# Softmax weights by tanh, and the accumulator read in the first slot of a tile

## What is computed

```python
def block(xb):                       # 128 tokens
    q = (xb @ w_q).reshape(p, 8, 2, 64)
    sc = jnp.einsum('phcd,hcnd->phcn', q, sub_keys)        # two scores of 128 keys, 8 heads
    top_s, top_i = lax.top_k(sc, 16)
    cand_s = top_s[:, :, 0, :, None] + top_s[:, :, 1, None, :]     # 256 pairs
    best_s, best_pos = lax.top_k(cand_s.reshape(p, 8, 256), 16)
    idx = take_along_axis(cand_i, best_pos)
    g = jax.nn.softmax(best_s, axis=-1)
    act = jax.nn.gelu(jnp.einsum('phkd,pd->phk', expert_u[idx], xb), approximate=False)
    return jnp.einsum('phk,phkd->pd', g * act, expert_v[idx])
```

## Time and profile before

| | |
|---|---|
| median of 3 runs | 1867.18 us (1865.82 to 1867.99) |
| profiled execution | 1864.53 us |
| its span | 1862.7 us |
| PE busy | 1598.0 us (86%) |
| DVE busy | 1501.8 us (81%) |
| POOL busy | 749.1 us (40%) |
| ACT busy | 427.5 us (23%) |
| mean DMA rate over the span | 335 GB/s |

### The profile page before, as it was taken

The page is one execution under the profiler, slowest core; times in us unless marked ns, Lnnn a source line. Parts: engine busy times, 40 slices in busy tenths (PEclk is TensorE's granted clock), DMA queues, the critical chain, the costliest instruction groups (busy, mean ns, idle before and its releaser), DMA issues.

```text
span 1862.7 us, 19074 instructions
## 1 busy us (share of the span) xinstructions
PE 1598.0 (86%) x4856; PEld 822.8 (44%) x4856; DVE 1501.8 (81%) x3370; ACT 427.5 (23%) x1040; POOL 749.1 (40%) x559
## 2 busy tenths in 40 slices
PE   8989999799978888887879888787888878888886
PEld 6878778677533333333333333333333333333332
DVE  5777886588768888888778888877888887888887
ACT  5223333354321211111211111121111112211111
POOL 1000000000014555655545666554556655555662
PEclk9999999899999999999989999999999999999999
DMA  8555472142239999999999999999999999999996
GB/s 305 181 215 180 160 277 95 51 169 80 91 119 393 421 421 422 422 422 421 409 400 409 422 422 422 421 402 397 413 422 422 422 422 389 422 422 422 422 422 254
DMA packets 93689, 623.97 MB, mean 335 GB/s; under 512 B 11441, under 2 KB 11441, under 8 KB 24241
## 3 DMA queue, kind: packets, MB, share of 16 engines
q0 software_dynamic: 78912, 570.46, 74.6%
q1 hardware_dynamic: 14704, 52.74, 7.8%
HBM read 621.06 MB, written 2.10 MB: 335 GB/s over the span
## 4 chain that ended last, share of the span: by engine, by line
DMA 34%; PE 30%; DVE 15%; DVEq 9%; issue 7%; ACT 4%; POOL 1%; POOLq 0%; ACTq 0%; SPq 0%
DMA arena<-in_experts,idx 32%; PE ps L624 8%; PE ps L412 6%; PE ps L413 6%; PE ps L414 6%; DVE arena L1303 5%; DVEq L1188 4%; PE ps L544 3%; DVE arena L1323 2%; POOL arena L401 1%; DVEq L1204 1%; DMA arena<-in_w_ada 1%; ACT L832 1%; PE ps L575 1%; ACT L836 1%
## 5 line engine op out<-in xcount | busy, mean ns | idle before, releaser
L624 PE MATMUL ps<-arena 128*128 128x512 f32 x2048 | 1017.0, 624 | 220.8 <-DVE arena L1323 198.7
L401 POOL DMA_INDIRECT arena<-in_experts,idx x512 | 727.9, 1422 | 767.7 <-PE ps L624 445.0
L624 PEld LDWEIGHTS ps<-arena 128*128 128x128 f32 x2048 | 356.1, 192 | 833.0 <-DVE arena L1323 548.5
L1303 DVE CUSTOM_DVE_ANT_0 arena<-arena,ada 128x1024 f32<-128x1024 f32 x512 | 627.4, 1225 | 88.6 <-DMA arena<-in_experts,idx 73.9
L832 ACT ACTIVATE arena<-arena 128x1 f32<-128x1 f32 x512 | 103.8, 203 | 1022.4 <-DVE arena L1303 1022.0
L1323 DVE TENSOR_SCALAR arena<-ident,arena 128x128 f32<-128x128 f32 x512 | 182.7, 357 | 48.0 <-ACT arena L832 43.0
L364 POOL DMA_DIRECT2D arena<-in_w_ada x24 | 12.9, 539 | 242.2 <-DVE arena L922 232.2
L412 PE MATMUL ps<-xT_hl,w_hl 128*128 128x512 f32 x192 | 78.1, 407 | 9.0 <-DVE xT_hl L886 9.0
L881 DVE TENSOR_TENSOR w_hl<-arena,w_hl 128x1024 fp32r<-128x1024 f32 x47 | 57.4, 1221 | 32.3 <-ACT w_hl L652 32.2
L413 PE MATMUL ps<-xT_hl,w_hl 128*128 128x512 f32 x192 | 76.2, 397 | 0.0
L414 PE MATMUL ps<-xT_hl,w_hl 128*128 128x512 f32 x192 | 75.9, 395 | 0.0
(11 more groups left out here) (223 smaller groups left out, 1693.3 us busy)
## 6 DMA issues: line engine op xcount, KB each, us to landing
arena<-in_w_ada POOLq DMA_DIRECT2D x24, 1024.0 KB, 5.2
arena<-in_w_in SPq DMA_DIRECT2D x44, 512.0 KB, 3.3
arena<-in_experts,idx POOLq DMA_INDIRECT x512, 14.6
arena<-in_w_out SPq DMA_DIRECT2D x14, 512.0 KB, 4.7
lnw<-in_w_in SPq DMA_DIRECT2D x8, 512.0 KB, 4.5
arena<-in_w_grp POOLq DMA_DIRECT2D x4, 1024.0 KB, 7.0
arena<-in_w_out SPq DMA_DIRECT2D x1, 4096.0 KB, 12.7
arena<-in_w_q SPq DMA_DIRECT2D x1, 4096.0 KB, 13.6
```

The source lines that it names most:

```text
L401: nc.gpsimd.indirect_dma_start(ring[:, n % RING, :], None, experts, bass.IndirectOffsetOnAxis(ap=idx[:, e, n:n + 1], axis=0)).then_inc(arr ...
L624: last = mm(ps[half][:, :], lhsT=diag[:, n % RING, :], rhs=ring[:, n % RING, DM + half * T:DM + (half + 1) * T], start=(e == 0 and n == 0) ...
L1303: nc.vector.tensor_tensor_reduce(out=urow, in0=urow, in1=h2cur, scale=1.0, scalar=0.0, op0=ALU.mult, op1=ALU.add, accum_out=dots[:, e, n:n ...
```

## The change

The softmax weight exp(x), with x = score minus the largest score, is written with the hyperbolic tangent: exp(x) = (1 + tanh(x/2)) / (1 - tanh(x/2)). ACT computes the tangent, DVE the quotient, the sum over 16 and the division by it (`gate_piece`, now in two pieces, in slots 7 and 8). The small pieces of DVE move: `pair_piece` 1 to 4 stand in slots 0 to 3, `index_piece` in 4 to 7, `key_piece` in 9 to 14, `pair_piece(0)` in 15. The query copy on ACT moves behind slot 4, the scores on PE behind slot 5, their copy on ACT behind slot 7. The output pieces 0 and 1 stand in slot 0 of the new tile instead of slot 1, and all output pieces stand ahead of the slot's diagonal instead of behind it. The mean square of the output is made in two halves after slots 1 and 2, the root after slot 5. At the end of the kernel pieces 0, 2, 1, 3 follow each other, and ACT squares the first half when it is ready.

```diff
             act.wait_ge(best_ready, 1)
-            nc.scalar.activation(best[:, :], best[:, :], ACT.Exp, accum_out=esum[:, :]).then_inc(exp_ready, 1)
+            nc.scalar.activation(best[:, :], best[:, :], ACT.Tanh, scale=0.5).then_inc(half_tanh, 1)
...
-                        if n == 4:
+                        if n == 5:
                             pe.wait_ge(q_copied, HEADS * t + h + 1)
                             pe.wait_ge(score_ready, 2 * HEADS * t + 2 * (h - 1))
...
+            def square_half(half, nth):
+                act.wait_ge(row_ready, nth)
+                c = slice(half * T, (half + 1) * T)
+                nc.scalar.activation(junk2[:, c], outb[:, c], ACT.Square, accum_out=stats[:, 13 + half:14 + half])
+                act.drain()
+                if half == 0:
+                    nc.scalar.activation(stats[:, 12:13], stats[:, 13:14], ACT.Identity, scale=1.0 / DM,
+                                         bias=stats[:, 15:16])
+            def root_of_halves():
+                act.drain()
+                nc.scalar.activation(stats[:, 14:15], stats[:, 14:15], ACT.Sqrt, scale=1.0 / DM,
+                                     bias=stats[:, 12:13]).then_inc(root_ready, 1)
...
+                    if row is not None and n in (1, 2):
+                        square_half(n - 1, row)
                     if n == 3:
+                        act.wait_ge(best_ready, step + 2)
+                        nc.scalar.activation(best[:, :], best[:, :], ACT.Tanh, scale=0.5).then_inc(half_tanh, 1)
+                    if n == 4:
                         copy_q(parity, 2 + parity, step + 3)
-                        act.wait_ge(best_ready, step + 2)
-                        nc.scalar.activation(best[:, :], best[:, :], ACT.Exp, accum_out=esum[:, :]).then_inc(exp_ready, 1)
-                    if n == 6:
+                    if row is not None and n == 5:
+                        root_of_halves()
+                    if n == 7:
                         act.wait_ge(score_mm, step + 3)
...
+            def gate_piece(piece, to):
+                plus, minus = tanhs[:, 0, :], tanhs[:, 1, :]
+                if piece == 0:
+                    ts(plus, best[:, :], 1.0, None, ALU.add)
+                    ts(minus, best[:, :], -1.0, 1.0, ALU.mult, ALU.add)
+                    dve.drain()
+                    nc.vector.reciprocal(minus, minus)
+                if piece == 1:
+                    dve.drain()
+                    nc.vector.tensor_tensor_reduce(out=plus, in0=plus, in1=minus, scale=1.0, scalar=0.0, op0=ALU.mult,
+                                                   op1=ALU.add, accum_out=esum[:, :])
+                    dve.drain()
+                    nc.vector.reciprocal(esum[:, :], esum[:, :])
+                    dve.drain()
+                    ts(gate[:, to, :], plus, esum[:, 0:1], None, ALU.mult)
...
             pair_piece(0)
-            pair_piece(1)
...
-            beside = {(0, 1): (0, 1), (0, 7): (2,), (0, 15): (3,), (1, 7): (4,), (1, 15): (5,)}
+            beside = {(0, 0): (0, 1), (0, 8): (2,), (0, 15): (3,), (1, 8): (4,), (1, 15): (5,)}
...
-                        if n < 3:
-                            pair_piece(n + 2)
-                        elif n < 7:
-                            index_piece(n - 3, 1 - e)
+                        if n < 4:
+                            pair_piece(n + 1)
+                        elif n < 8:
+                            index_piece(n - 4, 1 - e)
...
+                        if done is not None:
+                            for piece in beside.get((e, n), ()):
+                                output(done, piece)
                         dve.wait_ge(gelu_done, step * TOPK + n + 1)
                         ts(diag[:, n % RING, :], ident[:, :], acts[:, e, n:n + 1], gate[:, e, n:n + 1],
                            ALU.mult, ALU.mult).then_inc(diag_ready, 1)
-                        if done is not None:
-                            for piece in beside.get((e, n), ()):
-                                output(done, piece)
...
-            for piece in range(6):
+            for piece in (0, 2, 1, 3, 4, 5):
                 output(NT - 1, piece)
```

More of the change, by code:

```diff
@@ L205, in mixers_and_peer @@
         esum = sb("esum", [P, 1])
+        tanhs = sb("tanhs", [P, 2, TOPK])
         idx = sb("idx", [P, 2, TOPK], u32)
@@ L641, in _ @@
                             last.then_inc(score_mm, 1)
-                        if n == 5 and h == HEADS - 1:
+                        if n == 6 and h == HEADS - 1:
                             pe.wait_ge(h2n_ready, t + 1)
@@ L840, in act_step @@
                             nc.scalar.copy(cur[:, c, :], score_out(parity, c)).then_inc(score_ready, 1)
-                    if n == 2 and row is not None:
-                        root_of_squares(outb, junk2, row)
-                    if n == 9 and switch is not None:
+                    if n == 10 and switch is not None:
                         copy_h2T(switch + 2, 2)
@@ L857, in _ @@
                 act_step((NT - 1) * HEADS + e, e % 2, NT - 1 if e == HEADS - 3 else None)
-            root_of_squares(outb, junk2, 3 * NT)
+            square_half(0, 3 * NT)
+            square_half(1, 3 * NT + 1)
+            root_of_halves()
         @block.vector
@@ L1253, in _ @@
                 index_piece(piece, 0)
-            dve.wait_ge(exp_ready, 1)
-            gate_piece(0)
+            dve.wait_ge(half_tanh, 1)
+            gate_piece(0, 0)
+            gate_piece(1, 0)
+            dve.drain()
             make_h2(2)
```

32 lines of the change are left out of this document (14 added, 18 removed).

## The result

| | before | after |
|---|---|---|
| median | 1867.59 us (4 runs, 1865.82 to 1869.34) | 1898.43 us (4 runs, 1896.88 to 1899.81) |
| ratio after to before | | 1.0165, interval 1.0147 to 1.0183 |
| profiled execution, its span | 1864.53, 1862.7 us | 1898.01, 1896.2 us |
| DVE busy | 1501.8 us | 1520.6 us |
| ACT busy | 427.5 us | 344.4 us |

The changed kernel is 1.65% slower, 30.8 us by the medians. The forecast was 1858.1 us, range 1853.0 to 1864.0. What came is rival C, to which I gave 0.07.

The account below looks back on a forecast made before the run. It took the expert gathers' DMA rate, 422 GB/s, as the bound, with time lost only where gathers run short. Gains of 1.4 + 5.8 + 1.5 + 0.4 = 9.1 us off 1867.18 gave 1858.1 us, range 1853.0 to 1864.0.

Parts of the forecast that it names:

- rival C: DVE stalls at all eight inner-loop branches because the body grows: 31 us more, less 9.1, time 1889 us; chance 0.07.
- The inner branches, at nothing: DVE's branches back over two steps: no issue stall before, only 0.40 us for DMA, and no term in the sum.
- rival B: Only engines off the path get faster, so later releases gain nothing: no change, 1865.7 us; chance 0.12.
- Accumulator read: At a new tile's start, DVE reads the old accumulators in the first slot, PE starts 2.25 us earlier: 5.8 us won.
- Step 10: Behind the tile loop's branch back: branch pause stays, half the shortfall after slot 4 goes, 1.5 us for both places.
- Start: First slots of the expert stage: an index search leaves the way to the first dot, loads go; 1.4 us won.
- Table loads and new DVE work: Steady steps: removed ACT loads win nothing, and 1.0 us of new DVE work a step hides in free time.
- Tail: End of the kernel: half of the last square runs beside DVE, 0.63 us left instead of 1.06; 0.4 us won.
- step 8: Where the old tile's accumulators are read: gathers run short at three places, 7.44 us together.
- rival E: PE keeps its upper clock level after the shorter idle time at the accumulator read: 16 us won, 1851 us; chance 0.06.
- rival D: Tanh is not in gelu's table, so tables are still loaded: only 4.6 us won, time 1862.6 us; chance 0.02.

Follow-up runs that it names:

- a_pad32: The changed kernel with 32 empty DVE instructions (drains) ahead of the expert stage: 1867.08 us, ratio 0.9999 to the kernel before.
- b_read0: The kernel before with only the accumulator read and the output pieces moved as in the change: 1866.00 us, ratio 0.9993.
- b_tiles_read0: The kernel before with DVE's tile loop written out and the accumulator read in slot 0: 1859.94 us, ratio 0.9970.
- a_tiles: The changed kernel with 32 drains ahead of the expert stage and DVE's tile loop written out, inner loops kept: 1861.39 us, ratio 0.9964 to the kernel before.
- b_tiles: The kernel before with only DVE's tile loop written out, inner loops kept: 1859.04 us, ratio 0.9954.
- a_pad215: The changed kernel with 215 drains on DVE ahead of the expert stage: 1871.26 us, ratio 1.0028 to the kernel before.
- a_pad179: The changed kernel with 179 drains on DVE ahead of the expert stage: 1876.28 us, ratio 1.0060 to the kernel before.

## Why the prediction was wrong, point by point

**The inner branches, at nothing** are the step that failed: the sum has no term for them, and they cost 31 us. C's mechanism was named, with its place and price, and given 0.07 because "the free branch is half as long as the costly one, and the body grows by 5%". Both are true and neither decides. I compared lengths, where position decides, and counted 196 and 206 rows of the order, in which the drains (52 and 56), the match loads (18) and four semaphore instructions are missing: the body had 270 instructions and was, by the rule above, already long enough to be caught at some offsets. With a position not known, 27 starts in 256 for the first three tiles and as many for the last are some 0.2, against half that before. Its price was nearly right: 3.87 us an inner branch was forecast, 5.2 measured for six, 4.5 for two. Its sum of 1889 us was 9.4 short, since it took eight branches (31 us; six cost as much) less 9.1 us of gain that did not come. Without the pauses a_pad32 measures what rival B said, no change (1867.08 us, where B had 1865.7), and not the 1858.1 us of the forecast: the gain itself failed too, and the next points say where.

**Accumulator read, 5.8 us.** The mechanism was right and seen: PE idle for 2.43 us against the 2.8 expected, in the changed kernel and in a_pad32, windows at 422, 420 and 412 GB/s in a_pad32. As a gain in time it was over-sized: b_read0 gives 1.3 us (interval -0.7 to 3.4), and counted over the middle of the stage it is 1.2 with the tile branch and 1.9 and 2.7 without. What failed here is the adding up of shortfalls place by place, as if a place cured stayed won. In b_tiles_read0 a part of it is missing at the ends of the tiles, 80 us later; in a_tiles it is missing in a steady step. Why a place cured makes another short is open.

**Step 10, 1.5 us.** The 1.5 us did not come, and it went the other way: the windows at 960 and 1280 us are 372 and 371 GB/s in a_pad32, 381 and 383 before. My bounds, 0 and 3.0, left them no way to become worse.

**Start, 1.4 us.** Windows 48 to 88 us behind the stage's start are 3.3 us short in a_pad32 and 3.4 in the changed kernel, 3.5 before: 0.1 to 0.2. The timeline of the start in a_pad32 shows why releasing PE earlier bought so little (dots and gathers: start, us, idle before):

```profile
581.04 1.22 DVE L1339 CUSTOM_DVE_ANT_0 arena<-arena,ada 128x1024 f32<-128x1024 f32 x1
581.25 1.82 POOL L402 DMA_INDIRECT arena<-in_experts,idx  x1 [0.30 <-issue]
...
583.30 1.22 DVE L1339 CUSTOM_DVE_ANT_0 arena<-arena,ada 128x1024 f32<-128x1024 f32 x1
583.38 1.96 POOL L402 DMA_INDIRECT arena<-in_experts,idx  x1 [0.30 <-issue]
```

In the kernel before the gathers at 586.41 and 588.50 us lasted 1.19 and 1.30 us, behind 0.90 us of waiting for PE. With slots free, neither POOL (1.9 + 0.3 us a gather) nor DVE waits for another engine: the dots, too, start 2.1 to 2.3 us apart. Before, with POOL waiting 0.90 us each time, the gathers came 2.1 to 2.2 us apart as well. So DVE is enough to explain the pace, and whether POOL would hold it up too is not shown. A gather that starts within 0.25 us of a dot's start lasts 1.87 us in the median, in the kernel before and in the changed one; one that starts outside of any dot 0.94; those that start later in a dot lie between. The Trainium skill (GPSIMD Engine Reference, the row on SBUF interfaces) says that GpSimd shares its SBUF interfaces with VectorE, and contends for them with a VectorE instruction that has two SBUF inputs, as the dot has; the rows agree, and no run tried it. I had priced DVE and PE as pacers of a place that catches up, and left POOL out, which by these rows is as slow. That this is why the gain is lost in the middle of the stage too is argued, not shown.

**Table loads and new DVE work, nothing in a steady step.** Right. 8 loads are left in the stage, as forecast; the wait for the fifth gelu is gone; a window at 720 us of a_pad32 is at 422 GB/s with DVE at 34.51 of 40 us ("near 35"). The product with sum takes 177 ns, not 250. New work, loads gone and later query copy together cost 0.6 to 1.4 us over the stage by the table above, which is not told from nothing. The loads that went (most of 83 us of ACT) bought no time that the runs can tell.

**Tail, 0.4 us.** From PE's last end to the end of the span 9.5 us before, 9.3 after: 0.2. The second half of the square took 0.63 us, as forecast (timeline of the end, changed kernel):

```profile
1888.94 0.63 ACT L833 ACTIVATE arena<-arena 128x512 f32<-128x512 f32 x1 [0.30 <-DVE arena L1318]
```

**PE keeps its clock at step 8 (rival E).** Partly so. In a_pad32 the first four matmuls took 1.98 us after 2.43 us of idle time at two of the three step 8s (from 884.19 and 1209.57 us), and those windows are at 422 and 420 GB/s. At the third the clock fell to its lower level, and the window is at 412:

```profile
1534.68 5.40 PE L625 MATMUL ps<-arena 128*128 128x512 f32 x8 [2.44 <-DVE arena L1363]
```

The time that E promised for it did not follow, as for the read.

## What to carry to other kernels

When a change alters how many instructions an engine runs, count them as the engine executes them, drains and the extra loads that the trace shows included, for each loop body; by the rule above a body of more than 257 can stall at its branch at some offsets (270 to 336 long here, two of the four lengths did), and the same kernel with a few empty instructions ahead settles in one run whether it does. Here that was worth 31 us, more than anything the change meant to do, and writing out only the loop whose body is over 512 long was worth 8 us in the unchanged kernel. Where one shared rate (the gathers' DMA) bounds a stage, shortfalls cured place by place did not add up to time: sum the windows of the whole stage before and after, and ask who paces the recovery.

## What the runs showed of the hardware that I had not expected

- A held branch cost DVE 4.8 to 6.1 us while the gathers filled the DMA engines. Each cost the kernel 4.5 to 5.2 us at an inner branch and 4.1 at the tile branch (b_tiles, 8.2 us for two). One on ScalarE, 5.2 to 5.4 us long, cost no time that the runs can tell.
- Straight code was not free: with all DVE loops written out the kernel before ran 0.3% slower than with loops, and the changed one 0.6% slower than a_pad32, though no held branch was left on DVE.
- The tangent is in gelu's table: no load stands between the two in any step, against the list that the prediction cites for rival D.
- The stage began between 505.0 and 510.9 us without regard to the edit (a_pad215 and a_pad179 aside), with a granted TensorE clock of 0.92 to 0.94 from 350 to 400 us in the early ones and 0.88 to 0.89 in most late ones. Differences of under 0.2% between single profiles are of this size; I compared stages from their own start.
